# Two causal convolution layers: which engine begins the tap sums, and which tiles GpSimd sums

## The chip, the cores and the metric

The kernel runs on one core of one Trainium2 chip. The metric is device time of one execution, in microseconds (us). The profile names the engines PE (TensorE), DVE (VectorE), ACT (ScalarE), POOL (GpSimd) and SP (SyncE, which issues the loads). PEld is TensorE's weight load.

## The reference, cut to what matters

Four mixer layers and one further block work on 512 tokens of 1024 channels in float32. Layers 0 and 3 of the first block (`j` is 0 and 1 in the kernel) are of this kind, and only they are touched:

```
proj = h @ w_in                                   # 1024 -> 3 * 2048
val, glu_gate, z = split(proj, 3)
u = val * sigmoid(glu_gate)
u = causal_depthwise_conv(u, conv_w) + conv_b     # 31 taps per channel: out[t] = sum_k w[k] * u[t - 30 + k]
u = silu(layer_norm(u, ln_g, ln_b))
return (u * silu(z)) @ w_out
```

The 2048 channels are 16 tiles of 128 channels by 512 tokens, `U[0]` to `U[15]`.

## The kernel before, in words

Each engine runs its own instruction list in order, and waits on semaphores that the others raise. In a convolution layer all lists go through the same 33 slots. In slots 0 to 15 TensorE multiplies gate and value of one tile (two products of 24 matmuls each, because each float32 operand is split into a high and a low part: `HH` and `HL` for activations, `WH` and `WL` for weights). ScalarE takes the sigmoid of the gate and VectorE multiplies it with the value into `U[slot]`. From slot 16 TensorE computes one tile of z per slot (24 matmuls; `z_tensor`), and ScalarE its silu. ScalarE also splits the weights of the chunks to come (`WH<-WR`, `WL<-WR`), and GpSimd issues the DMA that forms their low part. TensorE starts gate and value of slot s only when `U[s - 2]` is there.

The 31 taps of a tile are summed in one of two ways, which a small planner (`conv_plan`) spreads over the slots. A tile of `CHAIN` is summed by VectorE in a PSUM bank, one `stt` (scalar_tensor_tensor: bank = U shifted * weight + bank) per tap; in the profile this is `L81 DVE ... ps<-AR,CW,ps`. Each tap waits for the tap before it of the same tile. The planner takes taps from two open tiles in turn where two are open. A tile of `POOL_TAPS` with the number `PAD` (30) is summed by GpSimd: ScalarE multiplies one tap into a ring of seven buffers (`AR<-AR,CW`, `SQ<-AR,CW`, `DG<-AR,CW`), and GpSimd adds it (`AR<-AR`, `AR<-AR,SQ`, `AR<-AR,DG`). A smaller number means that GpSimd sums so many of the taps and VectorE the others, and GpSimd adds the two parts. `room` is how many taps or adds go into a slot.

A chain has to be begun, since the first write to its bank must not add. Tiles 0, 1 and 3 are begun by ScalarE, which writes tap 30 into the bank (`ps<-AR,CW`). The other nine (`PE_BEGINS`) are begun by TensorE with taps 30 and 29 as matmuls against diagonal matrices, which ScalarE builds (`AR<-ident,CW`). Each of these two matmuls is two in the profile (`PE ps<-AR 128*128 128x512`).

A finished chain is copied out by ScalarE (`evacuate_scalar`, `ps,VB`). TensorE then transposes the tile (`turn_u`, L67) into bank 3, the last two tiles into banks 2 and 6, and VectorE takes the statistics over channels for the layer norm (`moments`, four `bn_stats` per tile). The transposes of a tile wait for the statistics of the tile before it in the same bank. After the last statistics come `bn_aggr`, a reciprocal root and two diagonal tiles `DG`. TensorE spreads these over the partitions, and the norm, the product with silu(z) and the output projection follow. Between the last transposes and this spreading TensorE computes z tile 14:

```
            for i in LATE_TURN:
                turn_u(pe, j, i)
            wait_chain_bank(pe, j, CHAIN[-1])
            for i in CHAIN[-4:]:
                pe.wait_ge(a_ev, j, i)
            z_tensor(pe, j, KE - 2)
            spread(pe, ("ln", j), 1, banks[4][:, :])
```

Of the kernel before, what the change touches and what calls it, by code (L numbers as in the profile page):

```python
# [120 lines left out]
def build_program(nc, x, a_norm, a_w_in, a_conv_w, a_conv_b, a_ln_g, a_ln_b, a_w_out, b_norm,  # L121
# [4 lines left out]
    with ctx:  # L126
# [738 lines left out]


        a_sig, a_u, a_zs = sig("a_sig"), sig("a_u"), sig("a_zs")
        a_diag, a_init_p, a_init_a, a_tap, a_ev = (sig(n) for n in ("a_diag", "a_init_p", "a_init_a", "a_tap", "a_ev"))
        a_prod, a_add, a_turn, a_mom = sig("a_prod"), sig("a_add"), sig("a_turn"), sig("a_mom")
        a_agg, a_mr, a_rb, a_mb = sig("a_agg"), sig("a_mr"), sig("a_rb"), sig("a_mb")  # L870
        a_ln, a_silu, a_out = sig("a_ln"), sig("a_silu"), sig("a_out")
# [6 lines left out]
        RING = len(PROD)  # L878
        N_TILES = halfs(HT) + SQS + [DGS[1], PROD[2], PROD[3], DGS[0]]
        REST = DGS[1]  # L880
        DIAG = [ar(A0 + 8 * T + i * P, P) for i in range(5)]
        MV, MRS = ST[:, 384:392], ST[:, 392:396]
        BY = MV.rearrange("p (b s) -> p s b", s=2)

        POOL_TAPS = {2: PAD, 4: PAD, 7: PAD, 10: PAD, 12: 24}
        CHAIN = [i for i in range(KE) if POOL_TAPS.get(i, 0) < PAD]
        PE_BEGINS = CHAIN[3:]  # L890
        LAST_TAP = {i: PAD - 2 if i in PE_BEGINS else PAD - 1 for i in CHAIN}
        BY_PE = [(i, k) for i in PE_BEGINS for k in (PAD, PAD - 1)]
        POOLED = sorted(POOL_TAPS)
        Z_LATE = 3

        def conv_plan():


            taps = {i: list(range(POOL_TAPS.get(i, 0), LAST_TAP[i] + 1)) for i in CHAIN}
            adds = {i: list(range(PAD)) if POOL_TAPS[i] == PAD else list(range(1, POOL_TAPS[i])) + [PAD] for i in POOLED}  # L900
            plan, begun, open_, ended, emptied, done, turned, pooled = [], 0, [], {}, {}, {}, [], []
            for slot in range(2 * KE + 1):
                rest = slot == 2 * KE
                at = {"begin": [], "tap": [], "evac": [], "start": [], "add": [], "turn": []}
                lately = slot >= KE and plan[-1]["turn"]
                ripe = [] if lately else sorted((i for i in done if done[i] + (3 if POOL_TAPS.get(i) == PAD else 1) < slot and i not in turned),
                              key=lambda i: done[i])
                at["turn"] = ripe[:1]
                turned += at["turn"]
                for i in CHAIN:  # L910
                    if i in ended and slot == ended[i] + (1 if ended[i] < KE - 1 else 2):
                        at["evac"].append(i)
                        emptied[i] = slot
                        if i not in POOL_TAPS:
                            done[i] = slot

                def begin():
                    i = CHAIN[begun]
                    free = begun < 4 or emptied.get(CHAIN[begun - 4], slot) < slot
                    return i if free and i + (i >= 2) <= slot else None  # L920

                while begun < len(CHAIN) and begin() is not None:
                    at["begin"].append(CHAIN[begun])
                    open_.append(CHAIN[begun])
                    begun += 1
                room = PAD * KE if rest else (15) if slot < KE else (7)
# [140 lines left out]
        def layer_a_tensor(pe, j):  # L1067
# [9 lines left out]
            for slot in range(2 * KE + 1):  # L1077
# [10 lines left out]
                    z_tensor(pe, j, slot - KE)  # L1088
                elif slot == 2 * KE - Z_LATE:
                    z_tensor(pe, j, KE - 3)  # L1090
                for i in PLAN[slot]["begin"]:
                    if i in PE_BEGINS:
                        pe.wait_ge(a_u, j, i)
                        wait_chain_bank(pe, j, i)
                        for k in (PAD, PAD - 1):
                            pe.wait_ge(a_diag, j, i, k)
                            pe.mm(chain_bank(i)[:, :], DIAG[BY_PE.index((i, k)) % 5], U[i][:, k:k + T], k == PAD,
                                  k < PAD).then_inc(a_init_p, j, i, k)
                for i in PLAN[slot]["turn"]:
                    turn_u(pe, j, i)  # L1100
            for i in LATE_TURN:
# [10 lines left out]
        def layer_a_vector(dve, j):  # L1112
# [10 lines left out]
            for slot in range(2 * KE + 1):  # L1123
# [6 lines left out]
                for n, (i, k) in enumerate(some):  # L1130
# [4 lines left out]
                    if k > POOL_TAPS.get(i, 0):  # L1135
                        dve.wait_ge(a_tap, j, i, k - 1)
                    else:
                        if i in PE_BEGINS:
                            dve.wait_ge(a_init_p, j, i, PAD - 1)
                        else:  # L1140
                            dve.wait_ge(a_init_a, j, i)
# [46 lines left out]
        def diagonals_scalar(act, j, i):
            for k in (PAD, PAD - 1):
                n = BY_PE.index((i, k))  # L1190
                if n >= 5:
                    act.wait_ge(a_init_p, j, *BY_PE[n - 5])
                act.act(DIAG[n % 5], ident[:, :], ACT.Copy, scale=conv_w(j, k, i)).then_inc(a_diag, j, i, k)

        def evacuate_scalar(act, j, i):
            act.wait_ge(a_tap, j, i, LAST_TAP[i])
            o = REST if i in POOL_TAPS else U[i][:, PAD:]
            act.act(o, chain_bank(i)[:, :], ACT.Identity, bias=a_vec("conv_b", j, i)).then_inc(a_ev, j, i)

        def begins_scalar(act, j, at):  # L1200
            for i in at["begin"]:
                n = CHAIN.index(i)
                if i not in PE_BEGINS:
                    act.wait_ge(a_u, j, i)
                    wait_chain_bank(act, j, i)
                    act.act(chain_bank(i)[:, :], U[i][:, PAD:], ACT.Copy, scale=conv_w(j, PAD, i)).then_inc(a_init_a, j, i)
                if n + 1 < len(CHAIN) and CHAIN[n + 1] in PE_BEGINS:
                    diagonals_scalar(act, j, CHAIN[n + 1])
# [1785 lines left out]
```

## Time and profile before

| | before |
|---|---|
| median of 3 runs | 2593.55 us |
| lowest, highest | 2592.87, 2595.41 us |
| span of the profiled execution | 2593.1 us |
| PE busy | 2550.1 us |
| DVE busy | 1509.1 us |
| ACT busy | 1231.1 us |
| POOL busy | 1514.3 us |
| granted TensorE clock, mean | 0.996 |

The runs list gives no separate time for the profiled execution beside its span. Its span lies 0.45 us under the median and within the three runs. Layer 0 takes its slots from about 24 to 305 us of the span, layer 3 from about 1441 to 1721 us.

### The profile page before, as it was taken

What the parts mean: (1) busy time and instruction counts of PE and PEld (TensorE: products, weight loads), DVE (VectorE), ACT (ScalarE), POOL (GpSimd) and SP (SyncE); (2) the same over time, 40 slices, a digit from 0 to 9 for tenths busy, and PEclk for the clock granted to TensorE, in tenths of its full rate; (3) what the DMA queues carried; (4) which work ended last, traced back from release to release, by engine and by line L of the source; (5) the groups of instructions that cost most, each with busy time, mean ns of one, the idle gap of its engine ahead of it and who ended that gap; (6) DMA issues with size and microseconds to landing.
All of it is one profiled execution on the core that took longest, in us unless ns stands there. A gap on an engine that the chain in (4) does not pass through costs nothing.

```text
span 2593.1 us, 31711 instructions
## 1 busy us (share of the span) xinstructions
PE 2550.1 (98%) x12043; PEld 2055.1 (79%) x12043; DVE 1509.1 (58%) x2434; ACT 1231.1 (47%) x1944; POOL 1514.3 (58%) x935
## 2 busy tenths in 40 slices
PE   8999999999999999999999999999999999999998
PEld 6777787878778788888888887878876778788887
DVE  6999764165585714444450799976498744532202
ACT  5887645254564623222232588664335553422322
POOL 2999766444444366444455399966635547644653
PEclk9999999999999999999999999999999999999999
DMA  8776434434234133333333677543422242233221
GB/s 195 177 177 145 122 97 91 98 82 82 75 71 74 57 98 93 96 95 96 96 95 97 152 167 175 140 114 108 113 96 86 67 139 97 86 98 98 98 98 65
DMA packets 296440, 279.12 MB, mean 108 GB/s; under 512 B 17814, under 2 KB 258672, under 8 KB 296289
## 3 DMA queue, kind: packets, MB, share of 16 engines
q1 hardware_dynamic: 281472, 223.94, 31.0%
q0 software_dynamic: 14816, 53.16, 10.0%
q8 instruction: 96, 1.57, 0.2%
q14 instruction: 56, 0.45, 0.1%
HBM read 228.75 MB, written 5.84 MB: 90 GB/s over the span
## 4 chain that ended last, share of the span: by engine, by line
PE 82%; DVE 9%; ACT 4%; issue 2%; DMA 2%; POOL 1%; SPq 0%; DVEq 0%; POOLq 0%; ACTq 0%
PE ps L64 80%; DVE AR L81 4%; DVE AR L73 2%; PE ps L67 2%; DVE HL L81 1%; DMA WR<-in_a_w_in 1%; ACT L70 1%; ACT AR L70 1%; DMA WL<-WR 1%; ACT HT L70 1%; DVE X L73 1%; POOL AR L73 0%; DVE ps L81 0%; ACT WL L70 0%; ACT HH L70 0%
## 5 line engine op out<-in xcount | busy, mean ns | idle before, releaser
L73 POOL TENSOR_TENSOR WL<-WR,WH 128x1024 fp32r<-128x1024 f32 x324 | 818.8, 2547 | 762.6 <-ACT WH L70 762.6
L64 PE MATMUL ps<-HH,WH 128*128 128x512 f32 x3080 | 1226.7, 399 | 4.3 <-ACT HH L70 1.2
L64 PE MATMUL ps<-HL,WH 128*128 128x512 f32 x3080 | 1194.9, 391 | 1.3 <-DVE HL L81 1.3
L64 PE MATMUL ps<-HH,WL 128*128 128x512 f32 x3080 | 1096.1, 390 | 2.3 <-DMA WL<-WR 2.3
L64 PEld LDWEIGHTS ps<-HH,WH 128*128 128x128 f32 x3080 | 579.6, 188 | 146.6 <-issue 15.3
L64 PEld LDWEIGHTS ps<-HL,WH 128*128 128x128 f32 x3080 | 580.0, 188 | 127.0 <-issue 7.9
L64 PEld LDWEIGHTS ps<-HH,WL 128*128 128x128 f32 x3080 | 578.6, 188 | 123.8 <-DMA WL<-WR 2.7
L70 ACT ACTIVATE WH<-WR 128x1024 fp32r<-128x1024 f32 (+1 forms) x405 | 409.2, 1047 | 488.9 <-PE ps L64 443.0
L81 DVE SCALAR_TENSOR_TENSOR ps<-AR,CW,ps 128x512 f32<-128x512 f32 x654 | 454.6, 752 | 17.2 <-ACT ps L70 10.2
L73 POOL TENSOR_TENSOR AR<-AR 128x512 f32<-128x512 f32 x200 | 306.8, 1848 | 16.2 <-ACT AR L70 8.9
L70 ACT ACTIVATE AR<-ps 128x512 f32<-128x512 f32 (+3 forms) x265 | 131.9, 522 | 272.8 <-PE ps L64 176.5
L73 DVE TENSOR_TENSOR AR<-AR 128x512 f32<-128x512 f32 (+1 forms) x161 | 212.1, 1346 | 39.4 <-ACT AR L70 37.8
L64 PE MATMUL ps<-AR 128*64 128x128 f32 (+17 forms) x1450 | 216.6, 345 | 15.2 <-DVE AR L81 8.3
L73 DVE TENSOR_TENSOR HL<-AR,HH 128x512 fp32r<-128x512 f32 x57 | 76.1, 1346 | 197.4 <-ACT HH L70 192.5
L73 DVE TENSOR_TENSOR AR<-ps,HT 128x512 f32<-128x512 f32 (+1 forms) x70 | 47.7, 687 | 244.7 <-PE ps L64 224.5
L64 PEld LDWEIGHTS ps<-AR 128*128 128x128 f32 (+6 forms) x1450 | 132.1, 168 | 69.8 <-issue 41.3
L115 POOL DMA_DIRECT2D WL<-WR x81 | 105.7, 1305 | 69.7 <-ACT WL L70 69.7
L70 ACT ACTIVATE AR<-AR 128x512 f32<-128x512 f32 (+3 forms) x72 | 41.0, 588 | 198.4 <-DVE AR L73 192.0
L73 POOL TENSOR_TENSOR AR<-AR,SQ 128x512 f32<-128x512 f32 x80 | 132.3, 1899 | 1.3
L73 DVE TENSOR_TENSOR AR<-AR,HT 128x512 f32<-128x512 f32 x48 | 70.3, 1464 | 101.1 <-ACT AR L70 100.5
L73 DVE TENSOR_TENSOR X<-X,ps 128x512 f32<-128x512 f32 x48 | 32.4, 682 | 148.5 <-PE ps L64 148.3
L70 ACT ACTIVATE AR<-AR,CW 128x512 f32<-128x512 f32 x168 | 110.9, 713 | 2.5 <-POOL AR L73 2.5
(184 smaller groups left out, 2180.0 us busy)
## 6 DMA issues: line engine op xcount, KB each, us to landing
WR<-in_a_w_in SPq DMA_DIRECT2D x96, 512.0 KB, 5.2
WL<-WR POOLq DMA_DIRECT2D x81, 512.0 KB, 5.7
WR<-in_c_w_in SPq DMA_DIRECT2D x64, 512.0 KB, 5.4
WR<-in_a_w_out SPq DMA_DIRECT2D x16, 1024.0 KB, 4.9
WR<-in_b_w_in SPq DMA_DIRECT2D x16, 1024.0 KB, 8.4
WR<-in_b_w_in SPq DMA_DIRECT2D x32, 512.0 KB, 11.0
WR<-in_w_mlp_in SPq DMA_DIRECT2D x16, 1024.0 KB, 5.4
WR<-in_w_mlp_out SPq DMA_DIRECT2D x16, 1024.0 KB, 4.9
```

Of the source, the lines that this page charges most:

```text
L64: return Op(None if self.e is None else self.e.matmul(o, l, r, start=first, stop=last, skip_group_check=True))
L67: return Op(None if self.e is None else self.e.transpose(o, i, identity))
L70: return Op(None if self.e is None else self.e.activation(o, i, f, **kw))
L73: return Op(None if self.e is None else self.e.tensor_tensor(o, a, b, op))
L81: return Op(None if self.e is None else self.e.scalar_tensor_tensor(o, a, s, b, op0, op1))
L115: return Op(None if self.e is None else self.e.dma_start(o, i, accum_op=ALU.add))
```

## The change

No chain is begun by TensorE any more: the diagonals, their signals and the matmuls are gone, and ScalarE begins all twelve chains with tap 30. VectorE therefore adds tap 29 of nine more tiles. GpSimd now sums tiles 3, 5, 8 and 12 alone and shares tiles 0 (12 of its taps), 1 (6) and 11 (14); before, it summed 2, 4, 7 and 10 alone and shared 12 (24). The rooms of the planner change with it. `SHARED` guards the one buffer `REST` that all shared tiles use.

```diff
-        POOL_TAPS = {2: PAD, 4: PAD, 7: PAD, 10: PAD, 12: 24}
+        POOL_TAPS = {0: 12, 1: 6, 3: PAD, 5: PAD, 8: PAD, 11: 14, 12: PAD}
         CHAIN = [i for i in range(KE) if POOL_TAPS.get(i, 0) < PAD]
-        PE_BEGINS = CHAIN[3:]
-        LAST_TAP = {i: PAD - 2 if i in PE_BEGINS else PAD - 1 for i in CHAIN}
...
-            taps = {i: list(range(POOL_TAPS.get(i, 0), LAST_TAP[i] + 1)) for i in CHAIN}
+            taps = {i: list(range(POOL_TAPS.get(i, 0), PAD)) for i in CHAIN}
...
-                room = PAD * KE if rest else (15) if slot < KE else (7)
+                room = PAD * KE if rest else 14 if slot < 6 else 15 - (slot % 4 == 3) if slot < KE else 7 + slot % 2
...
-                room = PAD * KE if rest else (8) if slot < KE else (3 + slot % 2)
+                room = PAD * KE if rest else 8 - (slot % 4 == 3) if slot < KE else 3 + (slot % 3 == 0)
...
-                for i in PLAN[slot]["begin"]:
-                    if i in PE_BEGINS:
-                        pe.wait_ge(a_u, j, i)
-                        wait_chain_bank(pe, j, i)
-                        for k in (PAD, PAD - 1):
-                            pe.wait_ge(a_diag, j, i, k)
-                            pe.mm(chain_bank(i)[:, :], DIAG[BY_PE.index((i, k)) % 5], U[i][:, k:k + T], k == PAD,
-                                  k < PAD).then_inc(a_init_p, j, i, k)
...
         def evacuate_scalar(act, j, i):
-            act.wait_ge(a_tap, j, i, LAST_TAP[i])
-            o = REST if i in POOL_TAPS else U[i][:, PAD:]
+            act.wait_ge(a_tap, j, i, PAD - 1)
+            if i in SHARED and i != SHARED[0]:
+                wait_conv(act, j, SHARED[SHARED.index(i) - 1])
+            o = REST if i in SHARED else U[i][:, PAD:]
...
         def begins_scalar(act, j, at):
             for i in at["begin"]:
-                n = CHAIN.index(i)
-                if i not in PE_BEGINS:
...
+                act.wait_ge(a_u, j, i)
+                wait_chain_bank(act, j, i)
+                act.act(chain_bank(i)[:, :], U[i][:, PAD:], ACT.Copy, scale=conv_w(j, PAD, i)).then_inc(a_init, j, i)
```

What the planner makes of it, per layer:

| | before | after |
|---|---|---|
| taps on VectorE | 327 | 328 |
| of these, right behind a tap of the same tile | 88 | 113 |
| first, last slot with taps | 0, 28 | 0, 28 |
| adds on GpSimd | 144 | 152 |
| first slot with adds | 3 | 1 |
| matmuls that begin a chain | 18 | 0 |
| chains begun by ScalarE | 3 | 12 |
| diagonals built by ScalarE | 18 | 0 |
| products by ScalarE, with starts | 148 | 156 |

On TensorE, at the end of slot 6 of the first layer (difference, `ps<-AR` are the beginning matmuls of tile 5, `L67` the transposes of a finished tile):

```order
 L64 MATMUL ps<-HL,WH 128x512
 L64 MATMUL ps<-HH,WL 128x512 x8
-L64 MATMUL ps<-AR 128x512 x2
 L67 MATMUL ps<-ident,AR 128x128 x4
 L64 MATMUL ps<-HH,WH 128x512
```

The pair is gone and what stood behind it follows the gate and value products directly; this happens at nine places in each of the two layers.

On ScalarE, slot 1 and the first half of slot 2 of the first layer before (`AR<-ps` is the sigmoid, `ps<-AR,CW` a begun chain, `WH`, `WL` the weight split):

```order
L70 ACTIVATE WH<-WR 128x1024
L70 ACTIVATE WL<-WR 128x1024
L70 ACTIVATE AR<-ps 128x512
L70 ACTIVATE WH<-WR 128x1024
L70 ACTIVATE WL<-WR 128x1024
L70 ACTIVATE ps<-AR,CW 128x512
L70 ACTIVATE WH<-WR 128x1024
L70 ACTIVATE WL<-WR 128x1024
L70 ACTIVATE AR<-ps 128x512
```

and the same stretch after the change (`AR,CW`, `SQ<-AR,CW`, `DG<-AR,CW` are starts and products for GpSimd):

```order
L70 ACTIVATE AR<-AR,CW 128x512 x5
L70 ACTIVATE AR<-ps 128x512
L70 ACTIVATE WH<-WR 128x1024
L70 ACTIVATE WL<-WR 128x1024
L70 ACTIVATE ps<-AR,CW 128x512
L70 ACTIVATE SQ<-AR,CW 128x512 x2
L70 ACTIVATE DG<-AR,CW 128x512
L70 ACTIVATE AR<-AR,CW 128x512
L70 ACTIVATE WH<-WR 128x1024
L70 ACTIVATE WL<-WR 128x1024
L70 ACTIVATE AR<-AR,CW 128x512 x4
L70 ACTIVATE SQ<-AR,CW 128x512
```

Two starts and twelve products now stand in slots 1 and 2 up to the sigmoid of slot 2; of these, one start and four products stand ahead of the sigmoid of slot 1.

On VectorE, the end of the first layer's taps before (`L81` are taps, `L97` the statistics):

```order
L81 SCALAR_TENSOR_TENSOR ps<-AR,CW,ps 128x512 x21
L97 BN_STATS ST<-ps 128x6 x4
L81 SCALAR_TENSOR_TENSOR ps<-AR,CW,ps 128x512 x12
L97 BN_STATS ST<-ps 128x6 x16
L100 BN_AGGR ST<-ST 128x2 x4
```

and after:

```order
L81 SCALAR_TENSOR_TENSOR ps<-AR,CW,ps 128x512 x23
L97 BN_STATS ST<-ps 128x6 x4
L81 SCALAR_TENSOR_TENSOR ps<-AR,CW,ps 128x512 x2
L97 BN_STATS ST<-ps 128x6 x12
L100 BN_AGGR ST<-ST 128x2 x4
```

The statistics of tile 13 now stand ahead of the last two taps, and those of three tiles, not four, stand behind them.

## Rows read from the trace of the kernel before

**Rows 1.** The page: busy time of the engines

```profile
PE 2550.1 (98%) x12043; PEld 2055.1 (79%) x12043; DVE 1509.1 (58%) x2434; ACT 1231.1 (47%) x1944; POOL 1514.3 (58%) x935
```

**Rows 2.** Waits of TensorE, 28 to 305 us (total us, times, longest)

```profile
PE ps L64 <- DMA WL<-WR: 2.3, 1, 2.3
```

**Rows 3.** Timeline of TensorE, slot 12 of layer 0 (start us, us)

```profile
176.04 1.88 PE L64 MATMUL ps<-AR 128*128 128x512 f32 x4
177.76 0.60 PE L67 MATMUL ps<-ident,AR 128*128 128x128 f32 x4
```

**Rows 4.** Timeline of VectorE: slots 0, 1 and 9 of layer 0

```profile
40.84 11.84 DVE L81 SCALAR_TENSOR_TENSOR ps<-AR,CW,ps 128x512 f32<-128x512 f32 x15 [8.64 <-ACT ps L70]
...
63.26 0.69 DVE L73 TENSOR_TENSOR AR<-ps,AR 128x512 f32<-128x512 f32 x1
...
147.28 9.96 DVE L81 SCALAR_TENSOR_TENSOR ps<-AR,CW,ps 128x512 f32<-128x512 f32 x15
```

**Rows 5.** Waits of VectorE, 40.8 to 305 us

```profile
DVE ST L97 <- PE ps L67: 6.4, 3, 5.0
DVE AR L73 <- PE ps L64: 3.0, 2, 2.1
```

**Rows 6.** Waits of VectorE, 1453.7 to 1720.5 us

```profile
DVE AR L73 <- PE ps L64: 4.7, 3, 2.1
DVE ps L81 <- ACT ps L70: 1.6, 2, 0.8
```

**Rows 7.** Timeline of VectorE, last taps and statistics of layer 0

```profile
281.95 9.45 DVE L81 SCALAR_TENSOR_TENSOR ps<-AR,CW,ps 128x512 f32<-128x512 f32 x12
292.49 0.89 DVE L97 BATCH_NORM_STATS2 ST<-ps 128x6 f32<-128x128 f32 x4 [1.09 <-PE ps L67]
```

**Rows 8.** Timeline of VectorE, first and last taps of layer 3

```profile
1453.74 11.84 DVE L81 SCALAR_TENSOR_TENSOR ps<-AR,CW,ps 128x512 f32<-128x512 f32 x15 [0.77 <-ACT ps L70]
...
1467.65 9.31 DVE L81 SCALAR_TENSOR_TENSOR ps<-AR,CW,ps 128x512 f32<-128x512 f32 x14 [0.81 <-ACT ps L70]
...
1697.39 9.45 DVE L81 SCALAR_TENSOR_TENSOR ps<-AR,CW,ps 128x512 f32<-128x512 f32 x12
```

**Rows 9.** Chain that ended last, tail of layer 0 (start us, us, what)

```profile
292.45 5.47 PE ps L64 x24
297.92 0.45 PE ps L67 x4
...
298.40 2.49 DVE ST L97 x12
...
300.91 1.94 DVE ST L100 x4
...
305.27 1.13 PE ps L64 x2
```

**Rows 10.** Timeline of layer 3's tail: aggregation, and TensorE's spreading

```profile
1716.34 1.93 DVE L100 BATCH_NORM_AGGREGATE ST<-ST 128x2 f32<-128x96 f32 x4
...
1720.71 1.98 PE L64 MATMUL ps<-DG,ones 128*128 128x512 f32 x4 [0.57 <-DVE DG L73]
```

**Rows 11.** Stretches around TensorE's one longer stall (busy us; PEclk is the granted clock)

```profile
93.00:95.00 2.00, 1.85 (x7) 1.49 (x8) 1.89 (x4) 2.00 (x4) 2.00 (x3) 0.84 1.01 193
95.00:97.00 2.00, 2.00 (x6) 1.54 (x5) 1.93 (x3) 2.00 (x5) 2.00 (x3) 0.50 0.38 70
97.00:99.00 2.00, 2.00 (x9) 1.64 (x8) 1.93 (x4) 2.00 (x3) 2.00 (x3) 0.81 0.63 174
```

**Rows 12.** Timeline of ScalarE: sigmoid of slot 2, four products, layer 0

```profile
55.84 0.58 ACT L70 ACTIVATE AR<-ps 128x512 f32<-128x512 f32 x1
...
64.70 2.55 ACT L70 ACTIVATE AR<-AR,CW 128x512 f32<-128x512 f32 x4
```

**Rows 13.** Timeline of GpSimd: low-part DMA issues one slot apart

```profile
150.56 1.46 POOL L115 DMA_DIRECT2D WL<-WR  x1
...
161.82 2.00 POOL L115 DMA_DIRECT2D WL<-WR  x1
```

More of the change, by code:

```diff
@@ L867, in build_program @@
         a_sig, a_u, a_zs = sig("a_sig"), sig("a_u"), sig("a_zs")
-        a_diag, a_init_p, a_init_a, a_tap, a_ev = (sig(n) for n in ("a_diag", "a_init_p", "a_init_a", "a_tap", "a_ev"))
+        a_init, a_tap, a_ev = (sig(n) for n in ("a_init", "a_tap", "a_ev"))
         a_prod, a_add, a_turn, a_mom = sig("a_prod"), sig("a_add"), sig("a_turn"), sig("a_mom")
@@ L880, in build_program @@
         REST = DGS[1]
-        DIAG = [ar(A0 + 8 * T + i * P, P) for i in range(5)]
         MV, MRS = ST[:, 384:392], ST[:, 392:396]
         BY = MV.rearrange("p (b s) -> p s b", s=2)
-        POOL_TAPS = {2: PAD, 4: PAD, 7: PAD, 10: PAD, 12: 24}
+        POOL_TAPS = {0: 12, 1: 6, 3: PAD, 5: PAD, 8: PAD, 11: 14, 12: PAD}
         CHAIN = [i for i in range(KE) if POOL_TAPS.get(i, 0) < PAD]
-        PE_BEGINS = CHAIN[3:]
-        LAST_TAP = {i: PAD - 2 if i in PE_BEGINS else PAD - 1 for i in CHAIN}
-        BY_PE = [(i, k) for i in PE_BEGINS for k in (PAD, PAD - 1)]
         POOLED = sorted(POOL_TAPS)
+        SHARED = [i for i in POOLED if POOL_TAPS[i] < PAD]
         Z_LATE = 3
         def conv_plan():
-            taps = {i: list(range(POOL_TAPS.get(i, 0), LAST_TAP[i] + 1)) for i in CHAIN}
+            taps = {i: list(range(POOL_TAPS.get(i, 0), PAD)) for i in CHAIN}
             adds = {i: list(range(PAD)) if POOL_TAPS[i] == PAD else list(range(1, POOL_TAPS[i])) + [PAD] for i in POOLED}
@@ L1137, in layer_a_vector @@
                     else:
[L1138 to L1141, printed above, removed]
+                        dve.wait_ge(a_init, j, i)
                         dve.wait_ge(a_u, j, i)
@@ L1186, in layer_a_vector @@
             scaled_vector(dve, 3 * j, 3 * j + 1, va["norm_mix" if j else "b_norm"])
[L1188 to L1193, printed above, removed]
         def evacuate_scalar(act, j, i):
-            act.wait_ge(a_tap, j, i, LAST_TAP[i])
-            o = REST if i in POOL_TAPS else U[i][:, PAD:]
+            act.wait_ge(a_tap, j, i, PAD - 1)
+            if i in SHARED and i != SHARED[0]:
+                wait_conv(act, j, SHARED[SHARED.index(i) - 1])
+            o = REST if i in SHARED else U[i][:, PAD:]
             act.act(o, chain_bank(i)[:, :], ACT.Identity, bias=a_vec("conv_b", j, i)).then_inc(a_ev, j, i)
@@ L1201, in begins_scalar @@
             for i in at["begin"]:
-                n = CHAIN.index(i)
-                if i not in PE_BEGINS:
[L1204 to L1208, printed above, removed]
+                act.wait_ge(a_u, j, i)
+                wait_chain_bank(act, j, i)
+                act.act(chain_bank(i)[:, :], U[i][:, PAD:], ACT.Copy, scale=conv_w(j, PAD, i)).then_inc(a_init, j, i)
         def starts_scalar(act, j, at):
```

## The prediction

> **What bounds the kernel now.** I read the page first. TensorE is busy 2550.1 of 2593.1 us [rows 1], so anything taken off it looks like time won. Then the waits of TensorE in layer 0: over 28 to 305 us it has one wait of any size, 2.3 us for a low weight part [rows 2]. From slot 7 on it runs without a gap to the end of z tile 13. So in these layers TensorE is what the others wait for, and it has work that the change takes away.
>
> Next I asked how far VectorE is behind. Its waits for TensorE between its first tap and the aggregation are 3.0 us before the products `U` and 6.4 us before statistics in layer 0, of which 5.0 are one wait at the end [rows 5]; in layer 3 they are 4.7 us and again 6.4 us, and a chain that was not begun in time costs 0.8 us [rows 6]. That is all the time that VectorE has free: 9.4 and 11.9 us. Its work for the convolution is not reduced by the change. So VectorE is nearly a second bound, and the 5.0 us wait at the very end says that it finishes its taps shortly before TensorE finishes z tile 13: the last tap of layer 0 ends at 281.95 + 9.45 = 291.4 us [rows 7], TensorE gets to its last transposes at 297.9 us [rows 9].
>
> **TensorE's part.** A pair that begins a chain holds TensorE from 176.04 to 177.76, which is 1.72 us [rows 3]. Nine pairs are 15.5 us per layer, 31.0 us in all. Without any new wait TensorE would reach its last transposes in layer 0 at 297.9 - 15.5 = 282.4 us.
>
> **VectorE's part.** From its first tap on it can now run without waits for TensorE, and this sets the end. The first tap does not move: it waits for ScalarE's begin of tile 0 (8.64 us, to 40.84 [rows 4]), and nothing ahead of that changes. To the work between first and last tap comes:
> - One tap more (328 for 327). In turn on two tiles 15 taps take 9.96 us, so 0.66 us each [rows 4].
> - Taps right behind a tap of their own tile: 25 more (113 for 88). Fifteen of one tile take 11.84 us against the 9.96 us of fifteen in turn, with 14 such places [rows 4]: 1.88 / 14 = 0.134 us per place, 3.4 us in all.
> - Four statistics more stand ahead of the last tap: 12 take 2.49 us [rows 9], so four take 0.8 us.
>
> That is 4.9 us per layer. Layer 0: the end moves from 291.4 by -3.3 (waits of 3.0 and of 6.4 - 5.0 - 1.1 = 0.3 fall away [rows 5, 7]) and +4.9, to 293.0 us. Layer 3: the last tap ended at 1697.39 + 9.45 = 1706.8. There 4.7 + 0.3 us fall away, 4.9 come, and the wait for the begin of tile 1 grows by the 0.8 us of the tap that slot 0 lost, because this begin stood behind a late weight load and not behind VectorE [rows 6, 8]. That gives 1707.5 us.
>
> The Trainium skill ("VectorE: DVE Perf Modes", section on the DRAIN you can't avoid) says that every operation drains the pipe anyway and that a semaphore between them costs nothing extra. By it the 3.4 us would be nothing and the result 6.8 us lower than mine, about 2578. The two rows of fifteen taps speak against it, so the sum goes by them.
>
> **The tail.** Behind the last tap VectorE still has the statistics of tiles 14, 12 and 15. The first eight take 1.7 us; in that time ScalarE copies tile 15 out and TensorE transposes it (0.45 us [rows 9]); with the copy I take 1.3 us for both. So the aggregation starts 1.7 + 0.8 = 2.5 us behind the last tap: 295.5 for 300.9 in layer 0, 1710.0 for 1716.3 in layer 3 [rows 9, 10]. From there it is 4.4 us to the spreading of the norm on TensorE (300.91 to 305.27) by the path over VectorE: 299.9 and 1714.4.
>
> But z tile 14, which covered this time, now starts later. In TensorE's list it stands behind the transposes of tile 15, so it starts at 293.0 + 1.3 = 294.3. Its 24 matmuls take 5.5 us [rows 9], to 299.8, which is just in time at the full clock. The clock is the question. TensorE will stand idle for several us here: its transposes of tile 14 need the free bank, that is, the statistics of tile 13, which stand two taps ahead of VectorE's end (291.4), and TensorE could be there at 282. Behind the one stall of 2.3 us in layer 0 the granted clock was 0.84, 0.50 and 0.81 over three stretches of 2 us [rows 11]: 1.2 GHz instead of 2.4 for a while, which costs 0.3 + 1.0 + 0.4 = 1.7 us of matmul work. I charge this once per layer on z tile 14: 301.5 in layer 0 and 1708.8 + 5.5 + 1.7 = 1716.0 in layer 3.
>
> The Trainium skill ("TensorE: Matmul & The Clock Gate", Part 1) has the low clock as the state that an idle TensorE falls back to. It speaks against making TensorE wait, and the stall in the trace agrees.
>
> **The sum.** The spreading comes at 301.5 for 305.27 and at 1716.0 for 1720.71 [rows 9, 10]: 3.8 + 4.7 = 8.5 us. Nothing behind it is changed. Against the profiled span of 2593.1 this is 2584.6, and as the median of before lies 0.45 us above that span, 2585.0.
>
> **What is costed at nothing.** ScalarE: 18 diagonals fall away, nine begins, two starts and six products come, at 0.64 us each by the row of four [rows 12]. Its slots have spare time, but in slots 1 and 2 the order matters: eight products and one start now stand between the begin of tile 1 and the sigmoid of slot 2, or ahead of it, about 5.6 us. The sigmoid ended at 56.4 and VectorE needed it at 63.3 [rows 4, 12]; now it ends near 61.3 and is needed near 62.4. The cover is 1 us, and what is late beyond that moves VectorE's whole run. GpSimd: eight adds and two issues took 11.26 us per slot [rows 13]. A gate and value slot of TensorE is 2 x 5.47 = 10.9 us plus a transpose. With one add left out in each fourth slot GpSimd just keeps up, and it starts two slots sooner. Its eight extra adds end before VectorE's taps do.
>
> **Rivals.**
> - All of TensorE's 31.0 us come out: 2562.5. VectorE's free time of 21.3 us [rows 5, 6] speaks against it. A case between, where most of that free time is won (dependent taps cheaper than I charge, clock kept), lies at 2573 to 2578. Together 0.09.
> - The same chain with z tile 14 at the full clock: the gains are 305.27 - 299.9 and 1720.71 - 1714.4, 11.7 us, 2581.9. It is the lower part of my forecast's own range.
> - No difference: GpSimd and ScalarE are late in the first slots. If the adds of slots 1 and 2 delay the weights' low parts by four adds (4 x 11.26 / 8 = 5.6 us at most), the next load and the begin of tile 2 come as late, and VectorE stands still for 1 to 5 us per layer. That eats 2 to 10 us: 2587 to 2595. For it: ScalarE already waits for weights there [rows 8]. Against it: TensorE waits only once for a low part now [rows 2]. 0.24.
> - Slower: GpSimd becomes the bound of slots 8 to 15. By slot 15 TensorE is some 7 us ahead of VectorE (seven pairs less, 12.0 us, against some 5 us that VectorE gains itself by its 3.0 us of waits [rows 5] and fewer taps up to there), so this decides once the low weight parts come more than 7 us late in total, about 1 us per slot, and beyond that each us counts: with 2 us per slot over ten slots it is 13 us per layer, 2611; with 1.5 us, 2601. For it: 11.26 against 10.9 us. Against it: the seven-add slots. 0.10.
> - The forecast, VectorE bound, 2579 to 2588: 0.57.
>
> **From these to the numbers.** A change of 0.2% (5.2 us) is about what a measurement of this kernel can tell from none. Faster by more than that needs a median under 2588.3: the first two cases and nearly all of the forecast, 0.64. Within 0.2%: 0.25. Slower: 0.11. The range goes from 2578 to 2595, which leaves out some 0.09 on each side.
>
> **What the profile after would show.** If the steps are right: VectorE has no wait for TensorE before `U` products in slots 14 and 15 and its last tap ends near 293 and 1707 us, in spite of 31 us less work on TensorE. TensorE has waits for VectorE before transposes (L67) in the z slots and before tile 14's, several us each, and a clock near 0.5 behind them. The spreading matmuls come 3 to 5 us sooner per layer. Wrong would be: waits of VectorE's `U` products on a sigmoid (ACT AR) or of its taps on a begin (ACT ps) in slots 1 to 5, waits of TensorE on `DMA WL<-WR` in slots 6 to 15, or z tile 14 at the full clock.

## The result: slower by 0.19%, and where the time went

The changed kernel takes 2599.06 us (median of 20 runs, 2596.2 to 2601.56), the kernel before 2593.9 us in the runs beside it (20 runs, 2590.97 to 2598.79). The ratio is 1.0019, with a 95% interval from 1.0012 to 1.0025. The forecast was 2585.0 us and a range from 2578 to 2595: wrong in its sign, and outside the range. The profiled execution has a span of 2598.6 us against 2593.1 us.

The line of the page that answers to [rows 1], profile of the changed kernel:

```profile
PE 2527.8 (97%) x11971; PEld 2043.5 (79%) x11971; DVE 1513.8 (58%) x2436; ACT 1241.9 (48%) x1942; POOL 1537.1 (59%) x951
...
PE 65%; DVE 10%; POOL 9%; issue 6%; DMA 5%; ACT 5%; SPq 0%; DVEq 0%; POOLq 0%; ACTq 0%
PE ps L64 63%; POOL AR L73 8%; DVE AR L81 4%; DMA WR<-in_a_w_in 3%; DMA WL<-WR 2%; DVE AR L73 2%; PE ps L67 2%; ACT AR L70 1%; DVE HL L81 1%; ACT L70 1%; ACT WL L70 1%; ACT HT L70 1%; DVE X L73 1%; POOL WL L115 0%; ACT WH L70 0%
```

TensorE lost 22.3 us of busy time (31.0 had been forecast), so the work did go. But 8% of the chain that ended last is now GpSimd's tap additions (`POOL AR L73`). The waits of TensorE in layer 0, 28 to 305 us (us in total, times, longest), say where; they answer to [rows 2]:

```profile
PE ps L67 <- POOL AR L73: 6.9, 1, 6.9
PE ps L64 <- DMA WL<-WR: 6.8, 6, 2.0
PE ps L64 <- ACT AR L70: 2.8, 1, 2.8
PE ps L67 <- DVE ST L97: 2.2, 1, 2.2
```

One wait of 6.9 us for GpSimd before transposes (L67), six for low weight parts where there was one, and one of 2.8 us for the sigmoid of slot 2. The first stands at the end of the layer. Timelines of VectorE, TensorE and GpSimd there, which answer to [rows 7, 9]:

```profile
292.61 1.53 DVE L81 SCALAR_TENSOR_TENSOR ps<-AR,CW,ps 128x512 f32<-128x512 f32 x2
294.05 0.88 DVE L97 BATCH_NORM_STATS2 ST<-ps 128x6 f32<-128x128 f32 x4
301.49 1.74 DVE L97 BATCH_NORM_STATS2 ST<-ps 128x6 f32<-128x128 f32 x8 [6.56 <-PE ps L67]
303.26 1.93 DVE L100 BATCH_NORM_AGGREGATE ST<-ST 128x2 f32<-128x96 f32 x4
```

```profile
300.33 1.97 PE L67 MATMUL ps<-ident,AR 128*128 128x128 f32 x8 [6.87 <-POOL AR L73]
309.20 1.88 PE L64 MATMUL ps<-DG,ones 128*128 128x512 f32 x4
```

```profile
294.14 1.27 POOL L73 TENSOR_TENSOR AR<-AR,DG 128x512 f32<-128x512 f32 x1
295.36 2.36 POOL L73 TENSOR_TENSOR WL<-WR,WH 128x1024 fp32r<-128x1024 f32 x1
297.66 2.62 POOL L73 TENSOR_TENSOR AR<-AR 128x512 f32<-128x512 f32 x2
```

VectorE's last tap ends at 294.1 us, close to the forecast of 293.0. GpSimd's last add of tile 12 ends at 300.3 us; the transposes of tiles 12 and 15 start 0.05 us later, the aggregation at 303.26 (before 300.91 [rows 9]) and the spreading at 309.20 (before 305.27). Layer 3 repeats it: its waits of TensorE, 1430 to 1740 us, and its aggregation and spreading, which answer to [rows 10]:

```profile
PE ps L67 <- POOL AR L73: 5.6, 1, 5.6
PE ps L64 <- DMA WL<-WR: 4.4, 5, 2.2
PE ps L67 <- DVE ST L97: 3.5, 1, 3.5
```

```profile
1720.69 1.93 DVE L100 BATCH_NORM_AGGREGATE ST<-ST 128x2 f32<-128x96 f32 x4
...
1726.25 1.88 PE L64 MATMUL ps<-DG,ones 128*128 128x512 f32 x4
```

The spreading of layer 3 is 5.5 us later than before, all of the difference of the spans (2598.6 - 2593.1). Nothing behind it changed.

### The profile page after: what moved, and what is told of

Read it like the earlier page. It is cut to its first block, busy times and chain, and to the rows that moved or that the text cites. A ratio compares the mean times of both kernels' runs of the same rounds, so it can differ in the third digit from the quotient of the medians.

```text
span 2598.6 us, 31597 instructions
## 1 busy us (share of the span) xinstructions
PE 2527.8 (97%) x11971; PEld 2043.5 (79%) x11971; DVE 1513.8 (58%) x2436; ACT 1241.9 (48%) x1942; POOL 1537.1 (59%) x951
## 4 chain that ended last, share of the span: by engine, by line
PE 65%; DVE 10%; POOL 9%; issue 6%; DMA 5%; ACT 5%; SPq 0%; DVEq 0%; POOLq 0%; ACTq 0%
PE ps L64 63%; POOL AR L73 8%; DVE AR L81 4%; DMA WR<-in_a_w_in 3%; DMA WL<-WR 2%; DVE AR L73 2%; PE ps L67 2%; ACT AR L70 1%; DVE HL L81 1%; ACT L70 1%; ACT WL L70 1%; ACT HT L70 1%; DVE X L73 1%; POOL WL L115 0%; ACT WH L70 0%
## 5 line engine op out<-in xcount | busy, mean ns | idle before, releaser
L73 POOL TENSOR_TENSOR WL<-WR,WH 128x1024 fp32r<-128x1024 f32 x324 | 817.8, 2544 | 759.3 <-ACT WH L70 759.3
L81 DVE SCALAR_TENSOR_TENSOR ps<-AR,CW,ps 128x512 f32<-128x512 f32 x656 | 459.9, 749 | 20.5 <-ACT ps L70 12.0
L73 POOL TENSOR_TENSOR AR<-AR 128x512 f32<-128x512 f32 x206 | 301.7, 1663 | 10.9 <-DVE AR L73 1.9
L73 DVE TENSOR_TENSOR AR<-AR 128x512 f32<-128x512 f32 (+1 forms) x161 | 212.0, 1345 | 41.8 <-ACT AR L70 40.1
L64 PE MATMUL ps<-AR 128*64 128x128 f32 (+17 forms) x1378 | 182.6, 332 | 15.0 <-DVE AR L81 8.1
L73 DVE TENSOR_TENSOR HL<-AR,HH 128x512 fp32r<-128x512 f32 x57 | 76.2, 1347 | 197.4 <-ACT HH L70 192.5
L73 DVE TENSOR_TENSOR AR<-ps,HT 128x512 f32<-128x512 f32 (+1 forms) x70 | 47.7, 687 | 243.7 <-PE ps L64 225.2
L64 PEld LDWEIGHTS ps<-AR 128*128 128x128 f32 (+5 forms) x1378 | 118.4, 167 | 59.5 <-issue 32.9
L73 POOL TENSOR_TENSOR AR<-AR,SQ 128x512 f32<-128x512 f32 x84 | 127.8, 1652 | 5.9 <-ACT SQ L70 3.9
L73 DVE TENSOR_TENSOR AR<-AR,HT 128x512 f32<-128x512 f32 x48 | 70.2, 1462 | 101.1 <-ACT AR L70 100.6
L70 ACT ACTIVATE AR<-AR,CW 128x512 f32<-128x512 f32 x178 | 118.2, 712 | 10.5 <-POOL AR L73 10.4
L115 POOL DMA_DIRECT2D WL<-WR x81 | 91.4, 1134 | 53.9 <-ACT WL L70 53.9
L73 DVE TENSOR_TENSOR X<-X,ps 128x512 f32<-128x512 f32 x48 | 32.4, 681 | 148.5 <-PE ps L64 148.2
```

What stands on the lines that cost most here:

```text
L64: return Op(None if self.e is None else self.e.matmul(o, l, r, start=first, stop=last, skip_group_check=True))
L70: return Op(None if self.e is None else self.e.activation(o, i, f, **kw))
L73: return Op(None if self.e is None else self.e.tensor_tensor(o, a, b, op))
L81: return Op(None if self.e is None else self.e.scalar_tensor_tensor(o, a, s, b, op0, op1))
L115: return Op(None if self.e is None else self.e.dma_start(o, i, accum_op=ALU.add))
```

## The experiments

Theory A is what the traces above suggest: a layer ends with the last of VectorE's taps and GpSimd's adds, and the changed kernel ends with GpSimd's. The runs were taken in three groups, and the kernel before had medians of 2594.03, 2594.66 and 2594.05 us in them. The runs that are built on the kernel before have the guard `SHARED` of the change too, which does nothing where only one tile is shared. Each trace is of one execution, and its time is given where it lies far from the median.

**GpSimd leaves out eight products of tile 12.** ScalarE leaves out the products that feed them too.

```
+            adds[12] = adds[12][8:]
```

> The kernel after the change, but GpSimd leaves out eight of tile 12's thirty adds (taps 0 to 7 of that tile are not in its sum, nor made by ScalarE). Theory A, GpSimd's last tile sets the end of both layers: after the change tile 12's last add ends at 300.3 us, VectorE's last tap at 294.1 us. Eight dependent adds of 1.37 us less bring GpSimd's end to about 289.5, so VectorE's last tap sets the end: the aggregation starts 2.5 us behind it, at about 296.6 instead of 303.3 in layer 0 and 1715.2 instead of 1720.7 in layer 3. About 11 us less in all, near 2588. Theory B, the end is set by TensorE's waits for low weight parts and for a sigmoid in the first slots: these stay, so the time moves by less than 2 us, near 2598.

Measured: 2589.58 us, ratio 0.9981 (0.9972 to 0.9991), 9.5 us under the changed kernel. VectorE and TensorE at the end of layer 0 (timelines):

```profile
290.63 1.53 DVE L81 SCALAR_TENSOR_TENSOR ps<-AR,CW,ps 128x512 f32<-128x512 f32 x2
292.06 1.67 DVE L97 BATCH_NORM_STATS2 ST<-ps 128x6 f32<-128x128 f32 x8
294.09 0.89 DVE L97 BATCH_NORM_STATS2 ST<-ps 128x6 f32<-128x128 f32 x4 [0.35 <-PE ps L67]
295.01 1.93 DVE L100 BATCH_NORM_AGGREGATE ST<-ST 128x2 f32<-128x96 f32 x4
```

```profile
300.99 1.98 PE L64 MATMUL ps<-DG,ones 128*128 128x512 f32 x4 [0.61 <-DVE DG L73]
...
1712.52 1.98 PE L64 MATMUL ps<-DG,ones 128*128 128x512 f32 x4 [1.46 <-DVE DG L73]
```

The wait for GpSimd is gone, and what comes is the forecast's own tail: aggregation at 295.0 (forecast 295.5), spreading at 301.0 (301.5), and in layer 3 8.2 us sooner than in the kernel before (8.5). The profiled execution is one of the faster ones of this kernel, 2586.72 us; beside the median the gain is smaller. The six waits for low parts are still there (6.2 us, longest 1.8), so they were not what cost the tail.

**TensorE begins none, but the old sharing stays.** This kernel computes everything.

```
-        PE_BEGINS = CHAIN[3:]
+        PE_BEGINS = []
```

> One part of the change alone: ScalarE begins all chains, TensorE none, but GpSimd keeps the tiles and the rooms that it had before (VectorE 336 taps, GpSimd 144 adds). Theory A: VectorE's last tap moves from 291.4 by minus 3.3 (waits) and plus 9 taps of 0.66 us to 294.0, GpSimd's last add of a tile stays at 294.7, TensorE's work ends far sooner. The aggregation starts near 297 instead of 300.9; with z tile 14 at half clock for a while the gain is 3 to 4 us per layer: about 2587, 7 us under the kernel before. Theory C, the idle TensorE (clock, z tile 14 uncovered) costs what its missing work gives: 2594 or more, and z tile 14 takes 7 us or longer.

Measured: 2590.64 us, ratio 0.9987 (0.9978 to 0.9996). The half of the change that takes TensorE's pairs away makes the kernel faster, by less than expected. GpSimd's last add ends at about 294.8 us here as before, TensorE waits 3.6 us for it, and the aggregation starts at 298.2. VectorE's last tap (293.8) is where theory A had put it.

**The new sharing, with TensorE's begins kept.** This one computes everything, too.

```
-        POOL_TAPS = {2: PAD, 4: PAD, 7: PAD, 10: PAD, 12: 24}
+        POOL_TAPS = {0: 12, 1: 6, 3: PAD, 5: PAD, 8: PAD, 11: 14, 12: PAD}
         (and the change's numbers of taps and adds for each slot)
```

> The other part alone: GpSimd's tiles and all rooms as after the change, but TensorE begins nine chains again (VectorE 319 taps, GpSimd 152 adds). Theory A: GpSimd's end of tile 12 stays near 300.3 and 1717.7 us and sets the end, the 31.0 us of TensorE's matmuls hide beside it: the same as after the change, 2598 to 2600. Theory B (TensorE late in the first slots and then bound): its 15.5 us per layer come on top of the stalls that it has now, last transposes near 306 us, about 2605 or more.

Measured: 2601.8 us, ratio 1.0028 (1.0017 to 1.004), 7.8 us over the kernel before. So the slowdown belongs to the sharing (its tiles and its rooms, which were not told apart). GpSimd's last add ends at 301.1 us and TensorE waits 2.4 us for it, as theory A says; the time is 1.8 us above its range. The two halves add up within the noise: -3.4 and +7.8 give +4.4, and both together gave +5.2. By theory A the second half alone should have been as slow as both; it came out 2.7 us slower, and the two 95% intervals overlap.

**GpSimd leaves out the products of tiles 0 and 1**, sixteen adds per layer, and ScalarE the products that feed them.

```
+            adds[0], adds[1] = [PAD], [PAD]
```

> The kernel after the change, but GpSimd leaves out its eleven and five adds of taps for tiles 0 and 1 (they are not in those sums), and keeps the two closing adds: its head start in slots 1 to 3 is gone, what it does from slot 4 on is the same. Theory D, the head start delays the low weight parts and by them the loads and ScalarE: TensorE's waits for low parts between 70 and 125 us and the one for the sigmoid at 61 us go, ScalarE's wait of 5.9 us for weights at 86 us shrinks, GpSimd's adds from slot 4 on start 4 to 6 us sooner and tile 12 ends at 294 to 296: about 2590. Against it, GpSimd's pace from slot 4 to 28 is set by its own count of adds: tile 12 ends at 299 to 300 as now, 2598.

Measured: 2591.59 us, ratio 0.999 (0.9981 to 0.9999). TensorE waits for low parts 1.4 us for 6.8, but still 4.2 us for GpSimd at the end, whose last add ends at 296.3 us for 300.3. That is still 1.6 us later than in the kernel before, with eight adds fewer than there. VectorE's way to the start of the statistics behind its last tap shrank from 242.3 to 240.0 us in layer 0 (from the `U` product of slot 1) and from 257.6 to 254.3 in layer 3 (from that of slot 0). In the changed kernel these 2.1 and 3.2 us are waits for ScalarE in slots 8 to 14: in layer 0 0.60 us for the begin of a chain at 134.79 and 1.52 us for a sigmoid at 188.44. Ahead of this sigmoid ScalarE had waited 4.55 us for a weight load (to 178.50 us) and then worked without a break. Without the early adds VectorE has none of these waits.

**Sixteen products of tile 12 left out**, and **tile 12's eight with the sixteen of tiles 0 and 1**.

```
+            adds[12] = adds[12][16:]
```

```
+            adds[0], adds[1], adds[12] = [PAD], [PAD], adds[12][8:]
```

> The changed kernel, with GpSimd leaving out 16 of the tap products of tile 12 (e1_drop12 left out 8). Theory A: with 8 left out VectorE's last tap (292.1 us in layer 0) is already last, so 8 more bring nothing: the time of e1_drop12 within 1 us, 2589 to 2590.5 us, and the aggregation at 295 us again. Theory B2 (every add of GpSimd counts, through the weights' low parts that its queue issues between the adds): 8 adds brought 9.5 us, so 16 bring about as much again: 2580 us.

> The changed kernel, with GpSimd leaving out 8 of tile 12 and the 16 of tiles 0 and 1 (e1_drop12 and e4_no_head together). Theory A: VectorE's last tap ended at 292.1 us in the one and 292.3 us in the other, so together nothing is won over the better of the two: 2588 to 2590.5 us, while TensorE's waits for low weight parts (6.2 us in six in the one, 1.4 us in two in the other, layer 0) stay near the 1.4 and its wait for VectorE's statistics grows instead. Theory B3 (the two gains have different places and add up): 2599.1 - 9.5 - 7.5 = 2582 us.

Measured: 2588.87 us (ratio 0.9972, 0.9961 to 0.9984) and 2584.43 us (0.9957, 0.9945 to 0.997). The first is theory A's by its median: once VectorE's last tap is last, fewer adds bring nothing. (Its six times lie apart, two at 2583.3 and 2584.0 us and four from 2588.8 to 2589.9; what tells them apart is not known. The trace is of one of the short ones, 2583.99 us.) The second is not: 5.2 us under the run with eight left out, most of the way to a sum. (The two were taken on different chips, and the executions that were traced, 2584.43 and 2586.72 us, are 2.3 us apart.) The aggregations of layer 0 and layer 3, first of eight left out with all else kept, then of both:

```profile
295.01 1.93 DVE L100 BATCH_NORM_AGGREGATE ST<-ST 128x2 f32<-128x96 f32 x4
...
1706.52 1.93 DVE L100 BATCH_NORM_AGGREGATE ST<-ST 128x2 f32<-128x96 f32 x4
```

```profile
294.82 1.93 DVE L100 BATCH_NORM_AGGREGATE ST<-ST 128x2 f32<-128x96 f32 x4
...
1704.10 1.93 DVE L100 BATCH_NORM_AGGREGATE ST<-ST 128x2 f32<-128x96 f32 x4
```

Layer 0 ends alike, layer 3 2.4 us sooner. Behind slot 1 of layer 3 VectorE waits for ScalarE in the changed kernel (3.2 us) and in all six variants of it that keep the early adds (0.5 to 3.1 us), and not at all in the two without them. In layer 0 the run with sixteen of tile 12 left out keeps the early adds and has no such wait: its way is 240.0 us, as without them. So the early adds go with a cost to VectorE in layer 3; for layer 0 this is not shown. My theory A left this out.

**Are slots 1 and 2 too crowded, or slots 8 to 15?** Both with sixteen products of tile 12 left out, and no other add taken away, only moved to other slots (the line of the changed kernel, and the two that took its place):

```
-                room = PAD * KE if rest else 8 - (slot % 4 == 3) if slot < KE else 3 + (slot % 3 == 0)
+                room = PAD * KE if rest else 6 if slot < 4 else 8 - (slot % 4 == 3) if slot < KE else 3 + (slot % 3 == 0)
```

```
+                room = PAD * KE if rest else 7 if 8 <= slot < KE else 8 - (slot % 4 == 3) if slot < KE else 3 + (slot % 3 == 0)
```

> The kernel of e7_drop12_16 (changed kernel, GpSimd leaves out 16 tap products of tile 12), and GpSimd's adds of slots 1, 2, 3 in the numbers 6, 6, 5 instead of 8, 8, 1; all later slots as there. Theory C (the crowded slots 1 and 2 delay low weight parts, with them the loads, ScalarE's splits and sigmoids, and so VectorE itself): TensorE's wait before the gate of slot 2 (2.6 us at 60.95) and the first for a low part go, VectorE's stretch from the first product to the last tap in layer 3 shrinks from 257.3 us towards the 254.3 of e8_drop_both, and the time falls towards that run: 2584 to 2587 us for 2588.9. Theory K (it is the number of adds ahead of slot 15, not their crowding): no difference, 2588 to 2590 us.

> The kernel of e7_drop12_16, with seven adds in every slot from 8 to 15 (there 8, 8, 8, 7), slots 1 to 7 as there. Theory C: slots 1 and 2 are as crowded as before, but the backlog of GpSimd is worked off from slot 8 on: waits of TensorE for low parts behind 150 us go, those at 72 and 140 us stay; half of the gain, 2586 to 2588.5 us. Theory L (the rival of the prediction: the steady rate in slots 8 to 15 is what delays VectorE): the whole difference to e8_drop_both comes back, 2584.5 us, and the sigmoid waits of VectorE in slots 12 to 14 of both layers go.

Measured: 2589.34 us (ratio 0.9981, 0.9972 to 0.999) and 2590.1 us (0.9984, 0.9975 to 0.9993), for 2588.87 without the move. Neither brings anything: not the crowding theory, and not the prediction's rival of slots 8 to 15. VectorE's way in layer 3, 257.3 us without the move, is 256.2 and 257.7. In the second TensorE's wait for the gate of slot 2 stays (2.9 us), one wait for a low part is 2.8 us long, and the sigmoid waits of VectorE (1.5 us in layer 0, 2.4 in layer 3) stay.

**The same move in the full changed kernel.**

> A whole kernel: the changed kernel with one number changed, so that GpSimd's adds of slots 1, 2, 3 come as 6, 6, 5 instead of 8, 8, 1. Theory C: GpSimd's idle time in slots 3 and 4 (3.0 us at 77.3 and 4.7 us at 88.2) mostly goes, and its last add of tile 12 ends 3 to 5 us sooner than 300.3; TensorE's 2.8 us at 61.1 goes. 2592 to 2595 us for 2599. Theory K (only the number of adds counts): 2598 to 2600 us.

Measured: 2597.98 us, ratio 1.0019 (1.001 to 1.0028), the changed kernel's. GpSimd's last add ends at 298.5 instead of 300.3 us, less than the 3 to 5 us expected, since its idle time mostly changed its place. Its longest waits between 24 and 310 us are now these:

```profile
POOL WL L115 <- ACT WL L70: 18.7, 6, 8.1
POOL AR L73 <- ACT AR L70: 5.5, 3, 5.0
```

The 5.0 us are a new wait for a product of ScalarE. VectorE's way did get shorter, by 0.7 us in layer 0 and by 2.1 us in layer 3 (255.5 for 257.6), but TensorE then waited 6.8 and 6.9 us for GpSimd. So the crowding theory fell here by its time; what it says of VectorE is neither shown nor refuted.

**Three versions that might be better**, all whole kernels. Tile 12 shared again (changed kernel, `12: 24`):

> The changed kernel with one number changed: GpSimd does 24 tap products of tile 12 as before the change and VectorE its last six and ScalarE its copy, instead of GpSimd all 30. Theory A: GpSimd's last add ends six adds or about 8 us sooner, near 292 us in layer 0 for 300.3, VectorE's last tap about 6 x 0.66 = 4.0 us later, at 298. The aggregation then starts about 2.5 us behind it, near 300.6 for 303.26, so 2.7 us per layer: about 2593.7 us. Theory G (VectorE has that much time free and only GpSimd counts): the gain of e1_drop12, 9 us: 2590 us. Theory H (tile 12 alone is not what matters): no difference, 2599 us.

Measured: 2594.86 us, ratio 1.0 (0.9991 to 1.0009). VectorE's last tap ends near 296.6 us and the aggregation starts at 299.48: GpSimd's load moved to VectorE, which is then last. This gives back nearly all that the changed kernel lost, and no more.

The kernel before with `PE_BEGINS = CHAIN[6:]`:

> The kernel before, with its sharing and its rooms, but TensorE begins only the last six of the twelve chains and ScalarE the first six. Theory A (each layer ends with whichever of three engines is last: TensorE's z tile 13, VectorE's last tap, GpSimd's last add): TensorE gets to its last transposes three pairs sooner, 297.9 - 3 x 1.72 = 292.7 us, VectorE's last tap ends near 292 to 293, and GpSimd's last add stays near 294.8 as in the run without any begins by TensorE. So GpSimd is last, as it was there, and the time is that run's within 1.5 us: 2589 to 2592 us. Theory F (TensorE's work counts as a sum): three pairs less in two layers are 10.3 us, but then the nine of e2_begin_only should have brought 31; scaled to what they did bring (3.4 us), three of nine would bring 1.1 us: 2592.9 us.

The kernel before with `PE_BEGINS = CHAIN[9:]` and `12: 22`:

> A whole kernel: the kernel before with TensorE beginning only its last three chains, and GpSimd doing 22 products of tile 12 instead of 24. Theory A (the last of VectorE's last tap and GpSimd's last add ends the layer): against e2_begin_only GpSimd ends two adds or 2.7 us sooner, at 292 us; VectorE has two taps more (1.3 us) and three less (2.1 us), and ends near 293 us. The aggregation starts near 296 us for 298.2 there, in two layers 4.4 us less: about 2586.5 us, range 2585 to 2589. Theory M (e2_begin_only's tail was bound by what stands behind the last tap, not by either engine): its time, 2590.6 us.

Measured: 2592.31 us (ratio 0.9991, 0.9982 to 1.0) and 2592.09 us (0.999, 0.9981 to 0.9999). Both missed. In the first I had GpSimd last again, and it is not: its last add ends at 294.9 us, and TensorE never waits for it. TensorE itself is last: it gets to its last transposes at 296.1 us and not at 292.7, after waits of 2.1 us for statistics and 1.8 us for a low part. The median is 0.3 us outside the range. So z tile 13 covers GpSimd's end again as soon as TensorE keeps six of its pairs. In the second no engine is late, but 4.5 us lie between VectorE's last tap (285.42 + 8.67 = 294.1) and the aggregation. VectorE's timeline of the second, end of layer 0:

```profile
285.42 8.67 DVE L81 SCALAR_TENSOR_TENSOR ps<-AR,CW,ps 128x512 f32<-128x512 f32 x11
294.39 0.89 DVE L97 BATCH_NORM_STATS2 ST<-ps 128x6 f32<-128x128 f32 x4 [0.30 <-PE ps L67]
296.09 2.48 DVE L97 BATCH_NORM_STATS2 ST<-ps 128x6 f32<-128x128 f32 x12 [0.81 <-PE ps L67]
298.61 1.93 DVE L100 BATCH_NORM_AGGREGATE ST<-ST 128x2 f32<-128x96 f32 x4
```

Sixteen statistics stand behind the last tap and wait for transposes in between, where the run without eight of tile 12 has twelve and 2.9 us. The old order of the last tiles has a longer tail, and I had taken the new one's. Of the whole kernels the one with the old sharing and no begins by TensorE has the lowest median, 2590.64 us, but its interval overlaps those of these two.

## Why the prediction was wrong, step by step

**The step that failed** is, in its own words, "Its eight extra adds end before VectorE's taps do", with "GpSimd just keeps up, and it starts two slots sooner" as its reason. I costed it at nothing and named no time at which GpSimd's last add ends. It ended at 294.7 us before, already behind VectorE's last tap (291.4) and hidden by z tile 13 alone, which ended at 297.9 us [rows 9]. The change took this cover away and gave GpSimd eight adds more. GpSimd's work (POOL, L73 and L115, 88.2 to 294 us), first before, then after:

```profile
L73 POOL TENSOR_TENSOR AR<-AR 128x512 f32<-128x512 f32 x75 | 117.1, 1982 | 1.3 <-ACT AR L70 0.7
L73 POOL TENSOR_TENSOR AR<-AR,SQ 128x512 f32<-128x512 f32 x36 | 60.2, 1942 | 0.5
L115 POOL DMA_DIRECT2D WL<-WR x27 | 41.1, 1521 | 0.0
L73 POOL TENSOR_TENSOR AR<-AR,DG 128x512 f32<-128x512 f32 x20 | 38.4, 1922 | 0.2
```

```profile
L73 POOL TENSOR_TENSOR AR<-AR 128x512 f32<-128x512 f32 x72 | 107.4, 1783 | 1.4
L73 POOL TENSOR_TENSOR AR<-AR,SQ 128x512 f32<-128x512 f32 x37 | 57.5, 1723 | 0.9
L115 POOL DMA_DIRECT2D WL<-WR x28 | 36.1, 1290 | 4.7 <-ACT WL L70 4.7
L73 POOL TENSOR_TENSOR AR<-AR,DG 128x512 f32<-128x512 f32 x19 | 32.7, 1722 | 0.4
```

Before, 131 adds (75, 36, 20) show in this stretch; the first was already running at 88.2 us, so 130 were left, and none lies behind. After, 128 lie in it and three end behind it: 131 were left. So of eight added adds the early start took off seven. The rest of the head start went in GpSimd's idle time between the early adds (3.7, 3.0 and 4.7 us, the last to 88.22): the first add from there on starts at 88.83 us, before it was 89.23. In the plan slot 3 has one add after two slots of eight: the head start was bounded there, and the order of the change could have told it.

From that add on GpSimd works almost without idle time in both kernels, for 211.4 us to the end of its last add where it was 205.4. Of these 6 us one more add is 1.25, and a weight split of 2.4 us now stands ahead of the last two adds (295.36). The rest is the order of the adds, which neither the prediction nor the experiments asked for: an add right behind an add of its own tile starts later than one behind an add of the other open tile. Three adds and the issue behind them, first before (tiles 7 and 4 in turn), then after (tile 12 alone):

```profile
141.22 4.06 POOL L73 TENSOR_TENSOR AR<-AR 128x512 f32<-128x512 f32 x3
144.96 1.16 POOL L115 DMA_DIRECT2D WL<-WR  x1
```

```profile
285.23 4.04 POOL L73 TENSOR_TENSOR AR<-AR 128x512 f32<-128x512 f32 x3
289.21 0.86 POOL L115 DMA_DIRECT2D WL<-WR  x1
```

The way is 3.74 us before and 3.98 after, 0.12 us for each of the two places. Behind an issue it is more: the add at 289.82 is followed at 291.46, 1.64 us later, where in turn it took 1.25 (145.57 to 146.82). The plan before has 28 adds per layer right behind one of their own tile in the same slot, the plan after 50, since one tile is open alone for longer and tile 12 is summed alone from slot 21 on. From the two traces I estimate 3.4 us per layer for these places (the 131 adds take 4.7 us more in all than the 130, from the start of each to the start of what follows, and 1.25 of that is the one more). About 1 us comes back in a wait of 0.7 us that is gone and in shorter issues. The prediction charged VectorE 3.4 us for just this (113 places for 88) and GpSimd nothing. No run changed this order alone, so its part is read from the traces and not tested.

**What it cost.** The forecast's spreading in layer 0 was 301.5 us and came at 309.2, 7.7 us late. Of these 1.1 us are VectorE's (294.1 for 293.0) and the rest stands behind GpSimd. The first product of layer 3 is 2.8 us later than before (1455.10 for 1452.28), so 1.1 of layer 0's 3.9 us came back in between, which no run explains. Layer 3's own spreading is 7.4 us behind the forecast. 7.7 - 1.1 + 7.4 = 14.0 us, and 2598.6 - 2584.6 is 14.0.

**What was right.** VectorE's term: from the product of slot 1 on to the last tap layer 0 was to take 240.4 us (52.59 to 293.0), and takes 240.0 where VectorE has no wait for another engine (three runs, two of them without the early adds) and 242.3 in the changed kernel, with its 2.1 us of waits for ScalarE. So 3.4 us for 25 more dependent taps was about right. By the Trainium skill's rule ("VectorE: DVE Perf Modes", section on the DRAIN you can't avoid) they would cost nothing, and an estimate by it leaves 237 us; the 240.0 us of the traces do not agree. TensorE as no bound: right, it is idle for 2.2 us before tile 14's transposes. The tail behind the last tap: 2.5 us forecast, 2.9 measured where GpSimd isn't last. The wait for the begin of tile 1 in layer 3 grew from 0.81 to 1.67 us, as forecast.

**The clock.** Stretches of the changed kernel (length, busy us of PE, PEld, DVE, ACT and POOL, then the granted clock), which answer to [rows 11]:

```profile
294.00:296.00 2.00, 0.00 (x0) 0.00 (x0) 0.93 (x5) 1.83 (x3) 1.92 (x3) 0.84 0.00 0
...
302.00:304.00 2.00, 2.00 (x7) 1.61 (x6) 1.97 (x8) 0.00 (x0) 2.00 (x2) 0.50 0.00 0
304.00:306.00 2.00, 2.00 (x7) 1.55 (x6) 1.66 (x6) 0.55 (x2) 0.92 (x1) 0.60 0.00 0
306.00:308.00 2.00, 2.00 (x10) 1.66 (x9) 1.72 (x7) 1.14 (x2) 0.00 (x0) 1.00 0.83 289
```

The clock falls to 0.50 (1.2 GHz) in the idle time and comes back behind 304 us. z tile 14 takes 6.9 us (302.3 to 309.2) for the 5.5 of z tile 13 before [rows 9]: 1.4 us, charged at 1.7. The tile ends after the norm's small steps are done, so the spreading, which was 4.4 us behind the aggregation, is now 5.9 us behind it in layer 0 and 5.6 in layer 3. The forecast had 6.0 (295.5 to 301.5), so this step was right, and its size too. The low clock as the state after idle time is also what the Trainium skill says ("TensorE: Matmul & The Clock Gate", Part 1).

**ScalarE and the rivals.** The cover of 1 us on the sigmoid of slot 2 was asked from the wrong side: VectorE did not wait for it, TensorE did, 2.8 us at 61.11 us. The sigmoid ended at 61.1 us, for 61.3 forecast. It cost nothing that shows at the end, since TensorE had time to spare. The rival of late low parts in the first slots (0.24, 2587 to 2595) had the size of VectorE's loss, 1 to 5 us per layer, and another place: its waits that go when the sixteen early adds go (2.1 and 3.2 us) lie in slots 8 to 14. The rival of slots 8 to 15 (0.10, GpSimd too slow by the steady rate, slower beyond 7 us of lateness) had the sign and the engine, and another place: TensorE waited 6.8 us for low parts in all and had the time to spare, and what decided was the end of the chain of adds, which no rival named. Nor are more adds needed for these waits: with the old sharing and no begins by TensorE there are six as well (6.4 us), and with the new sharing and TensorE's begins one of 0.2 us. They come where TensorE comes sooner, and without the early adds they fall to 1.4 us.

**What stays open.** Why VectorE waits 2 to 3 us more per layer for ScalarE with the sixteen early adds, and why the median without them is 5.2 us lower beside the run with eight left out, is not settled. The one late sigmoid that I followed stands behind a late weight load. Spreading the adds did not change the time, taking them away did, and with them go sixteen products of ScalarE; GpSimd's queue and ScalarE's were not told apart. Nor was it tested what GpSimd's last tile would cost with its adds in turn with another tile's.

## What to carry to other kernels

When work goes to an engine off the critical path, give that engine's last instruction a time of its own, and compare it with the time at which its cover ends after the change; busy shares and rates per slot don't show it. When a cover is taken away (here z tile 13, to 297.9 us), list everything that ended inside it: VectorE's taps at 291.4 us, which I listed, and GpSimd's adds at 294.7, which I did not. A head start counts only with what the schedule leaves behind it: count the operations from a fixed moment to the end, in both versions, and price what depends on the operation before it by the same rule on every engine.

## What the runs showed of the hardware

Not expected: of two stalls of TensorE one was three times as long as the other and cost only half as much again. Behind 6.9 us of it z tile 14 took 1.4 us more, and the eight transposes ahead of it took 1.97 us, where twelve took 1.47 us at the full clock (297.76 us in the kernel before). By the granted clock the whole is 1.8 us (0.50 from 300.3 to 304) and 0.8 us (0.60 to 306), an estimate of 2.6 us; by the same sum 2.3 us of idle time had cost 1.7 [rows 11].

The other is a price of GpSimd's: adds of one tile (128x512, float32) start 1.37 us apart, at 272.64, 274.01 and 275.38 us in the changed kernel, and adds of two tiles in turn 1.25 us apart, at 145.57 and 146.82 us in the kernel before. The last 28 adds of the changed kernel are all of tile 12, for 15 before.
